# The closing norm's shift row goes to the output early, and GpSimd's adding transfers bring the results

## What is computed

```python
h   = LayerNorm(alpha * x + mix, ln1_w, ln1_b)
ffn = moe_ffn(h, ...)                       # top 4 of 32 experts
out = layer_norm(alpha * h + ffn, ln2_w, ln2_b)

def layer_norm(x, w, b):
    xc = x - mean(x)
    var = mean(xc * xc)
    return xc * rsqrt(var + 1e-5) * w + b
```

## Time and profile before

| | us |
|---|---|
| median of 3 runs (lowest to highest) | 1284.54 (1284.0 to 1285.64) |
| span of the profiled execution, first to last instruction | 1282.2 |
| what the median has beyond that span | 2.3 |
| busy: PE / DVE / ACT / POOL | 1242.3 / 452.2 / 219.6 / 3.5 |
| read from HBM / written to it | 457.01 MB / 1.05 MB |

### The profile page before, as it was taken

The page is one execution under the profiler, slowest core; times in us unless marked ns, Lnnn a source line. Parts: engine busy times, 40 slices in busy tenths (PEclk is TensorE's granted clock), DMA queues, the critical chain, the costliest instruction groups (busy, mean ns, idle before and its releaser), DMA issues.

```text
span 1282.2 us, 14909 instructions
## 1 busy us (share of the span) xinstructions
PE 1242.3 (97%) x6126; PEld 643.6 (50%) x6126; DVE 452.2 (35%) x914; ACT 219.6 (17%) x430; POOL 3.5 (0%) x17
## 2 busy tenths in 40 slices
PE   9999999999999999999999999999998999899996
PEld 8888888998873343333333333333323333333332
DVE  5999924556342512121321213212121312122123
ACT  1722124231040110101111010110101010110102
POOL 0000000000000000000000000000000000000000
PEclk9999999999999999999999999999999999999999
DMA  9534344336979999999999999999999999999996
GB/s 380 204 134 152 109 154 160 114 110 223 424 280 408 429 432 426 435 431 429 433 429 434 432 429 433 429 434 432 429 433 429 434 430 430 433 428 428 428 424 260
DMA packets 31486, 458.70 MB, mean 358 GB/s; under 512 B 4785, under 2 KB 5169, under 8 KB 9426
## 3 DMA queue, kind: packets, MB, share of 16 engines
q1 hardware_dynamic: 27728, 453.00, 84.2%
q10 hardware_dynamic: 3714, 5.07, 1.2%
HBM read 457.01 MB, written 1.05 MB: 357 GB/s over the span
## 4 chain that ended last, share of the span: by engine, by line
PE 74%; DMA 16%; DVE 7%; ACT 1%; issue 1%; DVEq 0%; SPq 0%; POOL 0%; POOLq 0%
PE banks L1333 20%; PE banks L910 15%; PE banks L1369 14%; DMA store<-in_moe_w 13%; PE banks L1341 4%; PE banks L924 4%; DMA store<-in_w_last 3%; PE banks L1160 2%; PE banks L1185 2%; DVE store L2057 2%; PE banks L1440 2%; PE banks L1249 2%; PE banks L1351 1%; DVE store L2054 1%; DVE store L2051 1%; DVE store L2056 1%
## 5 line engine op out<-in xcount | busy, mean ns | idle before, releaser
L1333 PE MATMUL banks<-store 128*64 128x512 f32 x1536 | 342.6, 595 | 16.7 <-DMA store<-in_moe_w 16.6
L1333 PEld LDWEIGHTS banks<-store 128*64 128x64 f32 x1536 | 109.4, 137 | 231.9 <-issue 205.7
L1369 PE MATMUL banks<-store 128*64 128x512 f32 x952 | 210.9, 595 | 0.0
L910 PE MATMUL banks<-store 128*128 128x256 f32 x896 | 196.8, 380 | 0.0
L910 PEld LDWEIGHTS banks<-store 128*128 128x128 f32 x896 | 169.3, 190 | 26.4 <-issue 3.9
L2051 DVE TENSOR_SCALAR store<-banks 128x512 f32<-128x512 f32 x32 | 22.1, 692 | 428.8 <-PE banks L1341 428.8
L1369 PEld LDWEIGHTS banks<-store 128*64 128x64 f32 x952 | 65.9, 137 | 142.8 <-issue 120.1
L1341 PE MATMUL banks<-store 128*64 128x512 f32 x512 | 116.8, 598 | 0.4 <-DMA store<-in_moe_w 0.4
L2065 DVE COPY store<-banks 64x512 f32<-64x512 f32 x30 | 20.8, 694 | 203.3 <-PE banks L1369 203.3
L789 ACT ACTIVATE store<-store 128x512 f32<-128x512 f32 x28 | 17.6, 630 | 431.0 <-DVE store L2051 431.0
L1341 PEld LDWEIGHTS banks<-store 128*64 128x64 f32 x512 | 34.3, 136 | 70.1 <-issue 67.7
(11 more groups left out here) (380 smaller groups left out, 842.3 us busy)
## 6 DMA issues: line engine op xcount, KB each, us to landing
store<-in_moe_w SPq DMA_DIRECT2D x72, 4096.0 KB, 30.3
store<-in_moe_w SPq DMA_DIRECT2D x36, 2048.0 KB, 14.7
store<-in_w_in SPq DMA_DIRECT2D x30, 1024.0 KB, 4.8
store<-in_moe_w SPq DMA_DIRECT2D x18, 1024.0 KB, 9.3
store<-in_w_branch SPq DMA_DIRECT2D x8, 1024.0 KB, 4.8
store<-in_w_out SPq DMA_DIRECT2D x4, 1024.0 KB, 6.0
store<-in_w_last SPq DMA_DIRECT2D x4, 1024.0 KB, 34.8
store<-in_w_first SPq DMA_DIRECT2D x4, 256.0 KB, 4.3
```

The source lines that it names most:

```text
L910: last = mm(b[:, j * SEQ:(j + 1) * SEQ], w[:, k, j * P:j * P + P], xT[:, k, :], start=k == 0, stop=k == KD - 1)
L1333: last = mm(bank[into[i]][64 * ct:64 * ct + 64, :], xg[:, 2 * c + kk, col:col + CAP], w[:, kk, i * FF + ct * 512:i * FF + ct * 512 + 512], ...
L1369: last = mm(bank[4][64 * dh:64 * dh + 64, :], actT[:, j, 64 * fh:64 * fh + 64], w[j][:, 512 * dh:512 * dh + 512], start=(fh, j) == (0, 0), ...
```

## The change

`ln2_b` is no longer loaded into SBUF. Instead GpSimd, after its last memset, begins two transfers from HBM to HBM that write the row `ln2_b` into all 256 rows of the output. It then waits for both, waits for `out_ready`, and begins the three transfers of the results itself, with `accum_op=add`: each reads what stands in the output, adds the tile to it and writes the sum. DVE's last instruction of each piece only multiplies (`tensor_scalar`), and DVE waits for one row rather than two. SP waits at the end for all five transfers (`out_sent` at 80), as GpSimd does.

```diff
-        ln2_w, ln2_b = unit_at(LAST - 4)[:, 0:D], unit_at(LAST - 4)[:, D:2 * D]
+        ln2_w = unit_at(LAST - 4)[:, 0:D]
...
-            sp.dma_start(ln2_b, A["ln2_b"].to_broadcast([P, D])).then_inc(S["ln2_in"], 16)
...
-            sp.wait_ge(S["out_ready"], 1)
-            sp.dma_start(out[0][0:P, :], y_acc[:, 0, :]).then_inc(S["out_sent"], 16)
-            for dh in range(2):
-                sp.wait_ge(S["out_ready"], 2 + dh)
-                sp.dma_start(out[0][P:2 * P, 512 * dh:512 * dh + 512], y_acc[:, 1, 512 * dh:512 * dh + 512]).then_inc(S["out_sent"], 16)
-            sp.wait_ge(S["out_sent"], 48)
+            sp.wait_ge(S["out_sent"], 80)
...
             nc.gpsimd.memset(hg_s, 0.0).then_inc(S["hs_clear"], 1)
+
+            for half in range(2):
+                nc.gpsimd.dma_start(out[0][half * P:half * P + P, :], A["ln2_b"].to_broadcast([P, D])).then_inc(S["out_sent"], 16)
+            pool.wait_ge(S["out_sent"], 32)
+            pool.wait_ge(S["out_ready"], 1)
+            nc.gpsimd.dma_start(out[0][0:P, :], y_acc[:, 0, :], accum_op=ALU.add).then_inc(S["out_sent"], 16)
+            for dh in range(2):
+                pool.wait_ge(S["out_ready"], 2 + dh)
+                nc.gpsimd.dma_start(out[0][P:2 * P, 512 * dh:512 * dh + 512], y_acc[:, 1, 512 * dh:512 * dh + 512], accum_op=ALU.add).then_inc(S["out_sent"], 16)
+            pool.wait_ge(S["out_sent"], 80)
...
-            dve.wait_ge(S["ln2_in"], 32)
+            dve.wait_ge(S["ln2_in"], 16)
...
-                    V.scalar_tensor_tensor(y_acc[:, half, piece], h_tok[:, half, piece], small[:, 314 + half:315 + half], ln2_b[:, piece], ALU.mult, ALU.add)\
+                    V.tensor_scalar(y_acc[:, half, piece], h_tok[:, half, piece], small[:, 314 + half:315 + half], None, ALU.mult)\
                         .then_inc(S["out_ready"], 1)
```

## The result

The changed kernel takes 1291.4 us (median of 4, 1290.85 to 1292.68), the kernel before 1284.27 us (median of 4). The ratio is 1.0051, with a 95% interval from 1.0039 to 1.0063: slower by 0.5%, some 6.5 us (5.0 to 8.1 by the interval; the two medians lie 7.1 us apart). I had said 1286.3 and a range up to 1289.5; both are too low.

What follows compares the result with a forecast made beforehand. PE and the weight stream were taken as the bound, the edit acting only after PE's last product. First data at 1277.85, 5.32 us of data and 0.4 to landing meant 1.77 us later: 1284.54 + 1.77 = 1286.3 us, range 1284.0 to 1289.5.

Steps and rivals of the forecast that it cites:

- What was removed (0): Before the tail: dropping the load of ln2_b is worth 0, since PE's product still comes late.
- DVE's step: DVE's last step, multiplying only: 0.75 us for 1024 columns, 0.49 for 512; results 0.53, 0.79 and 1.05 us sooner.
- The early rows (0): Near 186 to 190 us: two 512 KB GpSimd transfers, 4.6 us or double, hidden behind busy PE; price 0.
- Slow issue: Rival at the output: each of three GpSimd issues takes over 1.9 us; at 2.5 us, 1288.8 us; chance 0.04.
- The issue (0.95 us and 0.45 to first data): GpSimd's output issue from 1276.45: 0.95 us, bounded by 0.34 and 1.03, then 0.45; first data at 1277.85.
- The data (5.32 us at 197 GB/s): Three adding output transfers, 1 MB end to end without a gap, at half of 394 GB/s, until 1283.17.
- the slow add: Rival at the output data: add sets the rate, under 171 GB/s; a third of 394 gives 1289.0 us; chance 0.25.
- From last data to the end (0.8 us): Kernel end: 0.4 us from last data to landing, barrier cost unchanged, GpSimd's drain 0, at most 1.0 us.
- some 3.5 us of DVE: Reading of the path after PE's last product: some 3.5 us of DVE, then issue, transfer, landing, barrier.
- DVE beside GpSimd: Claim that they hinder each other: DVE's 512-column copy took 0.79 us beside GpSimd's memset, a like one 0.43.

Runs made afterwards that it cites:

- the five versions without a wait: Changed kernel with doubled descriptor space, one add for the second half, two 64-row adds, early rows from SP, or eight early transfers: ratios 1.0028 to 1.0032.

## Why the prediction was wrong, point by point

**What was removed (0): right.** Without `ln2_b` DVE's wait for PE set the start as before: it waited 1.80 us for PE before its first addition of a piece, against 0.55 us.

**DVE's step: right.** 0.75 us for 1024 columns and 0.50 for 512, against 0.75 and 0.49. Counted from the start of the tail, the three results came 0.53, 0.79 and 1.07 us sooner, against 0.53, 0.79 and 1.05; 0.8 us arrive at the end.

**The early rows (0): right as a time, wrong as a whole.** I priced their bytes and their neighbours on the DMA engines. I didn't price what they leave behind: their places in GpSimd's descriptor space. That is the step that failed most clearly, and the one that puts the time outside my range: without the wait the tail is 4.1 us longer than before, which would make 1288.6 us. I wrote that nothing is queued behind GpSimd's waits, and that the three issues follow at 0.95 us each. The second did, the third had 4.59 us ahead of it and brought 2.3 us to the end. Slow issue was a rival with a chance of 0.04, but as three long issues; they took 0.93, 0.89 and 0.89 us, inside my bound. The number 1024 stands in the kernel's last function, and I never asked what it holds.

**The issue (0.95 us and 0.45 to first data): mis-sized by 0.7 us.** The issue itself took 0.93. But GpSimd began 0.60 us after DVE's first result (1276.76 to 1277.36), where SP took 0.03, and I had left that out. With the space doubled it was 2.1 us from the result (1277.32) to first data (1279.4), not 1.43; 0.57 us of that lie between the end of the issue and the data, where I had 0.45. The 0.95 I had got from GpSimd writing descriptors by program. The traces show of that only that the pages list its transfers under software_dynamic (q0, 720 packets in the changed kernel) and SP's under hardware_dynamic (q1), and the 0.93 us against SP's 0.34.

**The data (5.32 us at 197 GB/s): mis-sized by 1.3 us.** It was 6.6 us in the run with twice the space (1279.4 to 1286.0): 1048576 bytes at 159 GB/s. That is below the 171 GB/s that I had named as the point where the kernel becomes slower by over 0.2%, so the slow add was the true case, though not by the sum that I gave it (a third of the rate): 4 KB takes twice its former time by the median, 328 for 160 ns, but 391 ns by the mean in this run, and the longest, among the first, took 1.3 us in the changed kernel. Those slow packets are most of what lies between half the rate and the measured one. Half was my estimate; the median packet agrees with it, the whole transfer is at 0.40 of the plain 394 GB/s. That it is the second read is argued, not shown: the pages count 457.53 MB read from HBM with the add and without it.

**From last data to the end (0.8 us): mis-sized by 0.4.** In that run it is 1.2 us, from 1286.0 to 1287.2. The landing followed the last data by 0.3 us, as in the kernel before; from the landing to the end it took 0.9 us rather than 0.4, and GpSimd's drain, which I had put at 0, is 0.46 us of that (0.30 in the changed kernel).

So of the tail's 6.4 us my sum had 1.77; 0.7 + 1.3 + 0.4 = 2.4 us are terms that were too small (1.77 + 2.4 = 4.2, against 13.9 - 9.8 = 4.1 measured), and 2.3 us are a wait that I hadn't in any case.

One reading was wrong without bearing on the sum: between PE's last product and the issue I had counted some 3.5 us of DVE. By the earlier trace rows it is 7.4 us, from 1272.35 to 1279.79; only the last 4 us of it hold the changed instructions.

**DVE beside GpSimd: no delay seen.** I had read from the trace before that the two get in each other's way. That isn't shown: the copy of 0.79 us beside the memset is the only DVE copy of its kind there (`store` to `store`, 512 columns), it took 0.79 us beside the memset in the changed kernel too, and the 0.43 us were those of a `TENSOR_SCALAR`. At the end the second issue began at 1278.97, while the second multiplication still ran (it ended near 1279.07), so it was not held until then. The two overlap by 0.1 us only, so this is a weak test. Why the first issue lags by 0.60 us after a multiplication, and by 0.32 us in the run with plain transfers after the longer instruction (1277.37 to 1277.69), stays open.

## What to carry to other kernels

Ask of a transfer that moves to another issuer not only what its bytes cost but what the issuer does for each and which finite space that takes; the 1024 reserved in this program acted as such a space, and work 1093 us earlier had used it up. Count rows per transfer: fewer rows, another issuer or more space each took this wait of 4.59 us away. And an add inside a transfer at the very end trades here 0.8 us of DVE against 3.7 us of transfer and 1.0 us of issue from GpSimd, which have nothing left to hide them.

## What the runs showed of the hardware that was not expected

- GpSimd's descriptor space acts as if it filled in order with landed transfers keeping their places; the transfer that would pass the end waited 4.5 to 4.6 us. With the number at 1024 that was the third add after two early transfers, the second add after four, the eighth early transfer of eight; with 2048 none. The issues went on 0.3 to 0.4 us after the last transfer on the way had landed.
- An adding transfer of 128 rows takes GpSimd 0.86 to 1.01 us to issue where none follows at once, a plain one of results 0.54 to 0.68 us (SP: 0.34).
- Adding 1 MB in HBM from SBUF ran at 157 to 165 GB/s from first data to last in the five versions without a wait; plainly written 512 KB ran at 394.
- From GpSimd, plain transfers landed 2.3 to 3.0 us after the issue began (SP: 2.0 to 2.6), adding ones after 3.9 to 6.4 us.
